# Attention's q and k projected already turned, with the rotary halves moved to 32 partitions and back by DMA

## What is computed

```python
aq = partial_rotary(aq.reshape(B, S, n_heads, ATT_HEAD_DIM), pos)   # n_heads = 24, head 64, S = 512
ak = partial_rotary(ak.reshape(B, S, n_heads, ATT_HEAD_DIM), pos)
...
def partial_rotary(t, pos):
    half = ROT_DIM // 2                                             # ROT_DIM = 16
    ...
    r1 = tf[..., :half]
    r2 = tf[..., half:ROT_DIM]
    out = jnp.concatenate([r1 * cos - r2 * sin, r2 * cos + r1 * sin, tf[..., ROT_DIM:]], axis=-1)
```

## Time and profile before

| | |
|---|---|
| median of 3 runs | 1821.55 us (1821.44 to 1821.83) |
| the profiled execution | 1821.84 us |
| span of its instructions | 1820.0 us, so 1.84 us lie around it |
| TensorE busy in the span | 1790.7 us, 98% |
| VectorE, ScalarE | 1381.0 us (76%), 1100.2 us (60%) |
| `attention_stage`, to the last matmul of v0 | 213.5 to some 356 us from the start |

### The profile page before, as it was taken

How to read it: one execution, slowest core, us unless ns; L and a number is a source line. 1 busy time by engine, 2 the same in 40 slices (tenths; PEclk the granted TensorE clock), 3 DMA queues, 4 the chain that set the end, 5 groups by cost and what they waited for, 6 DMA issues and landing times.

```text
span 1820.0 us, 25032 instructions
## 1 busy us (share of the span) xinstructions
PE 1790.7 (98%) x9119; PEld 1472.9 (81%) x9120; DVE 1381.0 (76%) x1265; ACT 1100.2 (60%) x994; POOL 141.1 (8%) x120
## 2 busy tenths in 40 slices
PE   9999999999999999999999999999999999999996
PEld 7877788898888877788888888888888888888885
DVE  4256344337323568999999999999999999999997
ACT  4253222238331346777777777777777777777774
POOL 1000000000000017110000000000000000000001
PEclk9999999999999999999999999999999999999998
DMA  5321322211323558999999999999999999999993
GB/s 187 124 92 47 127 94 92 84 56 56 120 93 139 180 229 305 378 389 379 383 372 368 387 376 373 381 386 368 380 380 375 373 387 376 373 389 375 375 382 124
DMA packets 100601, 493.95 MB, mean 271 GB/s; under 512 B 15562, under 2 KB 17610, under 8 KB 51008
## 3 DMA queue, kind: packets, MB, share of 16 engines
q1 hardware_dynamic: 90640, 475.97, 68.3%
q0 software_dynamic: 9616, 16.62, 3.6%
q10 hardware_dynamic: 288, 0.59, 0.1%
HBM read 484.40 MB, written 25.21 MB: 280 GB/s over the span
## 4 chain that ended last, share of the span: by engine, by line
PE 58%; POOL 1%; DMA 1%; issue 1%; DVE 1%; ACT 0%; DVEq 0%; POOLq 0%
PE psum L1881 24%; PE psum L1894 12%; PE psum L1884 12%; PE psum L1899 6%; POOL slots_of_experts L1759 1%; PE psum L1853 1%; PE psum L1845 1%; PE psum L1874 1%; DMA h_sb<-normed_rows,row_index 1%; DMA slots_of_experts<-choice_token_and_weight,choice_row_of_table 0%; DMA lists_of_experts<-slots_of_experts 0%; DVE expert_chunk L2032 0%; DVE h_sb L2200 0%; DVE expert_lo L1729 0%; ACT expert_hi L1724 0%
## 5 line engine op out<-in xcount | busy, mean ns | idle before, releaser
L1729 DVE TENSOR_TENSOR expert_lo<-expert_chunk,expert_hi 128x2048 fp32r<-128x2048 f32 x384 | 865.7, 2284 | 45.2 <-ACT expert_hi L1724 42.6
L1724 ACT CAST expert_hi<-expert_chunk 128x2048 fp32r<-128x2048 f32 x384 | 734.9, 1916 | 225.8 <-PE psum L1884 187.6
L275 DVE TENSOR_TENSOR chunk_lo<-chunk,chunk_hi 128x2048 fp32r<-128x2048 f32 x48 | 109.9, 2290 | 252.9 <-ACT chunk_hi L271 252.7
L1881 PE MATMUL psum<-expert_hi,rowsT_hi 128*128 128x512 f32 x992 | 272.0, 396 | 0.0
L1884 PE MATMUL psum<-expert_lo,rowsT_hi 128*128 128x512 f32 x992 | 265.5, 389 | 0.5 <-DVE expert_lo L1729 0.5
L1881 PE MATMUL psum<-expert_hi,rowsT_lo 128*128 128x512 f32 x992 | 265.6, 389 | 0.0
L1884 PEld LDWEIGHTS psum<-expert_lo,rowsT_hi 128*128 128x128 f32 x992 | 186.1, 188 | 40.0 <-DVE expert_lo L1729 1.4
L1881 PEld LDWEIGHTS psum<-expert_hi,rowsT_lo 128*128 128x128 f32 x992 | 186.2, 188 | 39.6
L1881 PEld LDWEIGHTS psum<-expert_hi,rowsT_hi 128*128 128x128 f32 x992 | 181.5, 188 | 41.9 <-issue 7.6
L271 ACT CAST chunk_hi<-chunk 128x2048 fp32r<-128x2048 f32 x48 | 91.8, 1912 | 185.5 <-PE psum L306 158.1
L306 PE MATMUL psum<-chunk_hi,xT_hi 128*128 128x512 f32 x480 | 189.2, 394 | 4.3 <-ACT qk_rows_then_probsT L1070 1.7
(11 more groups left out here) (299 smaller groups left out, 1888.2 us busy)
## 6 DMA issues: line engine op xcount, KB each, us to landing
expert_chunk<-in_expert_w_gate_up SPq DMA_DIRECT2D x256, 1024.0 KB, 7.8
expert_chunk<-in_expert_w_down SPq DMA_DIRECT2D x128, 1024.0 KB, 6.9
chunk<-in_w_in SPq DMA_DIRECT2D x38, 1024.0 KB, 5.0
chunk<-in_w_branch_gla SPq DMA_DIRECT2D x4, 1024.0 KB, 5.0
chunk<-in_w_mix_out SPq DMA_DIRECT2D x4, 1024.0 KB, 5.1
gla_v<-in_x SPq DMA_DIRECT2D x4, 512.0 KB
y_glaT_away<-h_sb SPq DMA_DIRECT2D x1, 2048.0 KB, 7.7
att_qT_then_y_glaT<-y_glaT_away SPq DMA_DIRECT2D x1, 2048.0 KB, 7.6
```

The costliest lines, as they stand in the source:

```text
L275: dve.tensor_tensor(self.wlo[c][:], self.raw[c][:], self.whi[c][:].bitcast(F32), ALU.subtract).then_inc(self.lo_done[c], 1)
L1724: act.copy(self.expert_hi[c % self.SLOTS][:], self.expert_ring[c % self.RING][:]).then_inc(self.moe["hi"], 1)
L1729: dve.tensor_tensor(self.expert_lo[s][:], self.expert_ring[c % self.RING][:], self.expert_hi[s][:].bitcast(F32), ALU.subtract).then_inc(se ...
L1881: pe.matmul(bank, x[:, k, :], whi[s][:, m // 2, m % 2 * COLS:(m % 2 + 1) * COLS], start=False, stop=False)
```

## The change

The six q/k groups are multiplied with the weights stationary (`weights_stay`), as other groups of this kernel are, so a bank holds 128 columns on partitions and the 512 tokens along it. ScalarE copies the bank straight to `q`, `k` or `near`, sorted by residue where wanted (`out`). TensorE's transposes, VectorE's small rotations and its copies from banks 4 to 7 are gone.

The rotary halves now lie on four runs of 8 partitions (0, 8, 64, 72), where partners are on different partitions. So for each group, when its four banks are copied out, ScalarE's queue issues 8 DMAs of 8 partitions by 1024 numbers (`take_halves`, 32 KB each) that lay them out on 32 partitions in `halves`; VectorE multiplies with cosine and sine and adds, in four operations on 32 partitions (`rotate`); and SP issues 8 DMAs that put the result back (`put_halves_back`). The buffer `halves` is one, so the DMAs of group i wait until those that put group i - 1 back have landed (`put_back`). The cosine and sine and both products lie in `att_v`, which is not yet in use; ScalarE's first copy of v0 therefore waits for the sixth rotation (`rotated`).

```diff
@@ gla_stage, tensor engine
-                self.multiply_group(pe, base_att, self.block_of, between=last_turns)
+                self.multiply_group(pe, base_att, None, weights_stay=True, between=last_turns)
@@ attention_stage
+        halves = halves_and_pT[0:turning, :].rearrange("p (m n) -> p m n", n=SEQ)
+        rope, by_cos, by_sin = v[0:turning, 1], v[0:turning, 2], v[0:turning, 0]
+        places = ((q_near, 0), (q, 0), (q, HALF_KT), (k_near, 0), (k, 0), (k, HALF_KT))
...
+        def halves_of(i):
+            qk, at = places[i]
+            for h in range(2):
+                for tile in (0, 2):
+                    part = (h * 2 + tile // 2) * HALF
+                    for s in range(2):
+                        row = h * HEAD_DIM + s * HALF
+                        yield (qk[row:row + HALF, at + tile:at + tile + 2, :],
+                               halves[part:part + HALF, 2 * s:2 * s + 2, :])
@@ SP
-                sp.dma_start(rope[:], t["rope"].rearrange("(b p) n -> p b n", p=P)).then_inc(rope_in, 16)
+                sp.dma_start(rope, t["rope_T"]).then_inc(rope_in, 16)
...
-                with sp.Fori(2, 3 * G + 1) as i:
-                    self.load_group(sp, base + i, lambda c: self.w_in_chunk(COL_AQ + COLS * i)(c))
+                def load(i, c):
+                    sp.wait_ge(self.lo_done[c], base + i)
+                    sp.dma_start(self.raw[c][:], self.w_in_chunk(COL_AQ + COLS * i)(c)).then_inc(self.loaded[c], 16)
+
+                def put_halves_back(i):
+                    sp.wait_ge(rotated, i + 1)
+                    for rows, half_rows in halves_of(i):
+                        sp.dma_start(rows, half_rows).then_inc(put_back, 16)
+
+                load(2, 0)
+                load(2, 1)
+                load(3, 0)
+                for i in range(2 * G):
+                    put_halves_back(i)
+                    load(i + 3, 1)
+                    load(i + 4, 0)
+                load(3 * G, 1)
@@ tensor engine
-                with pe.Fori(1, 2 * G) as i:
-                    qk_group(i, lambda: turn_rows(i - 1))
-
-                self.multiply_group(pe, base_v, self.block_of, between=lambda: turn_rows(2 * G - 1))
+                self.run_groups("multiply", pe, base, (1, 2 * G), weights_stay=True)
+                self.multiply_group(pe, base_v, self.block_of)
@@ scalar engine
+                def out(i):
+                    qk, at = places[i]
+                    for b in range(NB):
+                        act.wait_ge(self.bank_full[b], base + i + 1)
+                        place, tile = qk[:, at + b, :], self.bank[b]
+                        if i % G:
+                            place, tile = place.rearrange("p (r n) -> p r n", r=RES), tile.rearrange("p (n r) -> p r n", r=RES)
+                        act.copy(place, tile).then_inc(self.bank_free[b], 1)
+
+                def take_halves(i):
+                    for b in range(NB):
+                        act.wait_ge(self.bank_free[b], base + i + 1)
+                    if i:
+                        act.wait_ge(put_back, 16 * MOVES * i)
+                    for rows, half_rows in halves_of(i):
+                        act.dma_start(half_rows, rows).then_inc(taken, 16)
+
+                out(0)
                 self.split_hi(act, base + 1, 1)
...
+                take_halves(0)
+                for i in range(1, 2 * G):
+                    self.split_hi(act, base + i + 1, 0)
+                    out(i)
+                    self.split_hi(act, base + i + 1, 1)
+                    take_halves(i)
...
+                    if i == 0:
+                        act.wait_ge(rotated, 2 * G)
@@ vector engine
+                def rotate(i):
+                    order = 2 if i % G else 0
+                    cos, sin = rope[:, order, :], rope[:, order + 1, :]
+                    dve.wait_ge(taken, 16 * MOVES * (i + 1))
+                    dve.wait_ge(rotated, i)
+                    dve.tensor_tensor(by_cos, halves, cos.unsqueeze(1).to_broadcast([turning, 4, SEQ]), ALU.mult).then_inc(products, 1)
+                    sines = sin.unsqueeze(1).to_broadcast([turning, 2, SEQ])
+                    dve.scalar_tensor_tensor(out=by_sin[:, 0:2, :], in0=halves[:, 2:4, :], scalar=-1.0, in1=sines,
+                                             op0=ALU.mult, op1=ALU.mult).then_inc(products, 1)
+                    dve.tensor_tensor(by_sin[:, 2:4, :], halves[:, 0:2, :], sines, ALU.mult).then_inc(products, 1)
+                    dve.wait_ge(products, 3 * (i + 1))
+                    dve.tensor_tensor(halves, by_cos, by_sin, ALU.add).then_inc(rotated, 1)
 
                 self.split_lo(dve, base + 1, 1)
...
+                for i in range(2 * G):
+                    self.split_lo(dve, base + i + 2, 0)
+                    rotate(i)
+                    self.split_lo(dve, base + i + 2, 1)
```

More of the change, by code:

```diff
@@ L61, in shape_constants @@
     cos, sin = np.cos(ang).astype(np.float32), np.sin(ang).astype(np.float32)
-    c["rope"] = np.concatenate([cos, cos, -sin, sin], axis=1).astype(np.float32)
+    by_residue = np.arange(SEQ).reshape(SEQ // RES, RES).T.reshape(-1)
+    c["rope_T"] = np.stack([np.tile(a[order].T, (ATT_HEADS // 2, 1)) for order in (np.arange(SEQ), by_residue) for a in (cos, sin)],
+                           axis=1).astype(np.float32)
     t, r = np.arange(P), np.arange(RES)
@@ L919, in attention_stage @@
         self.groups = base_gate = base_v + G
[L920 to L923, removed]
+        rope_in, taken, products, rotated, put_back, masks_in = (self.sem("att_" + n) for n in (
+            "rope_in", "halves_taken", "rope_products", "rotated", "halves_put_back", "masks_in"))
         q_near, k_near = near
@@ L969, in _ @@
             def _(pe):
[L970 to L978, removed]
                 def score(j):
@@ L1029, in values @@
                     last.then_inc(S["pv_done"], 1)
-                def qk_group(i, before=None):
-                    self.multiply_group(pe, base + i, self.block_of, between=before)
                 def gate_blocks(c, blocks):
@@ L1064, in _ @@
             def _(act):
[L1065 to L1070, removed]
-                self.split_hi(act, base + 1, 1)
[L1072 to L1083, removed]
+                def out(i):
[14 more added lines that the diff above has]
+                out(0)
+                self.split_hi(act, base + 1, 1)
+                take_halves(0)
[4 more added lines that the diff above has]
+                    take_halves(i)
                 def exps(m):
@@ L1129, in _ @@
                 dve.wait_ge(rope_in, 16)
[L1131 to L1156, removed]
@@ L1158, in _ @@
-                self.split_lo(dve, base + 1, 1)
-                rotate(0, q_near)
-                for first, qk in ((0, q), (G, k)):
-                    if first:
-                        for c in range(2):
-                            self.split_lo(dve, base + first + 1, c)
-                        rotate(first, k_near)
-                    with dve.Fori(1, G) as i:
-                        for c in range(2):
-                            self.split_lo(dve, base + first + i + 1, c)
-                        rotate(first + i, qk, i - 1)
+                def rotate(i):
[10 more added lines that the diff above has]
+                    dve.tensor_tensor(halves, by_cos, by_sin, ALU.add).then_inc(rotated, 1)
@@ L1188, in probs @@
                     dve.tensor_scalar(neg[u], neg[u], inv[:, u:u + 1], None, ALU.mult).then_inc(S["probs_done"], 1)
-                with dve.Fori(2 * G + 1, 3 * G) as i:
-                    for c in range(2):
-                        self.split_lo(dve, base + i, c)
+                for c in range(2):
+                    self.split_lo(dve, base_gate - 1, c)
                 self.split_lo(dve, base_gate, 0)
```

10 lines of the change are left out of this document (5 added, 5 removed).

## The result

The changed kernel takes 1829.5 us (median of 6 runs, 1828.2 to 1831.4) against 1821.5: a ratio of 1.0043, with a 95% interval of 1.0032 to 1.0053. It is slower by some 8 us, where 8 us less was forecast, and just above the range. The profiled execution took 1828.66 us with a span of 1826.9, so its own difference from before is 6.9 us of span; the medians lie 8.0 apart.

A forecast was written before the change was run, and what follows sets the result against it. TensorE, busy 98% of the span, was taken as the bound. From 1821.84 us, -10.6 for transposes and +2.5 for a new wait at v0 gave 1813.7, less 0.3: 1813.4 us; range 1811.3 to 1829.

The forecast's parts named there:

- What went: TensorE's 16 transposes in each of six q/k groups disappear, 1.77 us a group: -10.6 us.
- The rotation: VectorE's four rotation operations per group take 7.1 us; fewer partitions save nothing.
- The landing: The last of eight DMAs put back lands 2.1 us after its issue has passed; 3.5 instead would be worth +7.
- The issue price: Each small DMA issue on SP or ScalarE costs 0.50 us, so eight take 4.0 us; sixteen a lap.
- the text's own steepness: One more hundredth of a us per issue adds 0.16 us a lap and 0.64 + 0.16 at v0.
- The ring's form: Loop of rounding, rest, rotation, DMAs back, landing and DMAs out: 21.6 us a lap against TensorE's 21.76, just closing.
- its two outlets: TensorE waits at v0, +2.5 us; for chunk_lo in groups q1 to k2 only if the loop is over 6.5 late.
- rival 1: Issues into the ring cost 0.77 us each, lap 26.1 us, like loads into busy queues: 1835 us; chance 0.20.
- signs of being wrong: Eights of 5 us or more, take_halves waiting longer each group, or TensorE waiting for chunk_lo inside q/k groups.
- The start: First lap hangs on q2's chunk 0 load: rounding from 227.5, lateness 2.0 us at first, 1.3 at v0.
- The chances: Whole change: faster 0.68, slower 0.20, the same 0.12; the forecast's 1812 to 1816 had 0.56.
- The rule beside it: Skill page calls issue time usually small beside the DMA; that would give 8 us of room and 1812.1 us.

The follow-up runs named there:

- the run without any new wait: Changed kernel with halves-out DMAs on SP's queue, sine products in the attention-output tile and q2's first load ahead of the store: 1812.01 us, ratio 0.9943.
- run 8: Changed kernel with sine products in their own place and ScalarE's eight DMAs moved behind the next group's chunk 0 rounding: 1821.23 us, ratio 0.9993.
- run 1: Changed kernel with the sine products in the attention-output tile, so v0's first copy no longer waits for the sixth rotation: 1819.95 us, ratio 0.9987.
- run 2: Changed kernel with the eight DMAs out of q and k issued by SP instead of ScalarE: 1814.33 us, ratio 0.9951.
- run 5: Changed kernel with only the first head of each pair moved and rotated, four DMAs each way, timing only: 1812.64 us, ratio 0.9949.
- run 9: Changed kernel with sine products apart, ScalarE's DMAs behind the next rounding, and SP's loads held until the halves out landed: 1813.01 us, ratio 0.9948.
- run 4: Kernel before plus five sets of four 32 KB DMAs on SP: issues about 0.6 us SBUF to SBUF, 0.3 to 0.4 from HBM; no kernel time given.
- Run 3: Changed kernel with q2's chunk 0 load issued ahead of the tables, the 2 MB store and the masks: 1826.67 us, ratio 1.0023.
- run 7: Changed kernel with halves-out DMAs split four each on ScalarE and SP, sine products apart and q2's first load early: 1811.92 us, ratio 0.9945.

## Why the prediction was wrong

**What went: right.** 10.6 us were forecast for the transposes; the run without any new wait gained 10.8 in the stage.

**The rotation: right.** 7.1 us forecast; 234.65 to 241.5 is 6.9, on 32 partitions and on 16 alike.

**The landing: right, where nothing else is in flight.** 2.1 was taken; 1.8 is measured. That it may meet a load and land late was in the text as harmless, and in this kernel it was; in run 8, where the halves stand last in the ring, it cost 8 us.

**The issue price: the step that failed.** "I take 0.50: 4.0 us" came from rows that all had HBM at one end; the DMAs here, with SBUF at both ends, cost 0.66, and eight of them 5.3 us. By the text's own steepness, 0.8 us for each hundredth, 0.16 more is 12.8 us: 1826.2 for 1813.4. The ring's form and its two outlets (waits for `chunk_lo`, and the wait at v0) are what runs 1, 2, 5 and 9 confirm. It was rival 1 in effect, at a price between the forecast's and its own 0.77, but not for its reason. Full queues are not what made the issues dear: behind the first group all sixteen from `att_kT` took 0.631 or 0.632 us on ScalarE's queue, and SP's, with no load just ahead, a median of 0.625. The rival's remark that no row was a DMA from SBUF to SBUF was the right one; the 8 partitions in it were not what counted (run 4). Two of the signs of being wrong came, the eights of over 5 us and the waits for `chunk_lo`.

**The start: mis-sized.** q2's load was taken to land at 227.5; ScalarE got it at 230.5. Run 8, in which the first eight DMAs are issued only at 227.22, has it when the forecast said:

```profile
227.08 1.91 ACT L273 CAST chunk_hi<-chunk 128x2048 fp32r<-128x2048 f32 x1 [9.73 <-DMA chunk<-in_w_in]
```

So the eight DMAs in flight beside the load cost it 3.4 us, where 0.7 was allowed for them and the larger tables together; they were slow to issue there too (8.0 us from 215.73, for 5.3). Run 3 shows that a start is handed through one for one as far as v1's first matmul, so 3 us more: 1829.2.

**The clock: not in the sum.** After the 9.0 us idle TensorE ran at half its clock for some 3.5 us, 1.8 us lost. Price, start and clock together would give about 1831; the landing was 0.3 and the rotation 0.2 us quicker than forecast in each of five passes, which makes 1828.5, and the restarts, some 1 us, were not in the sum either. That is near the measured 1829.5; closer than 1 us this account does not go.

**The chances.** Twenty in a hundred for slower, at a point where one price unknown in the trace moved the time by 0.8 us per hundredth, was too little. The nearest rows were all of another kind (HBM at one end), and their spread of 0.43 to 0.52 was taken for the spread of the unknown. The bound on the other side, 0.77, was in the text, but with the argument against it that the transfers are small. In run 4 transfers of one size, 32 KB, cost 0.6 or 0.3 to 0.4 by where their ends lie.

**The rule beside it.** The page of the Trainium skill, "DMA: Bandwidth & Descriptors", section Issuing engines are not separate DMA queues, calls the sequencer's time for an issue usually small relative to the DMA. Here eight issues take 5.3 us and the last lands 1.8 later; the measurement decides. Its other half, that issuing from several engines saves only that time, agrees with run 7: the issues took 3.0 us in place of 5.3, and the time stayed.

## What to carry to other kernels

When work leaves the bounding engine, draw the ring that the new buffer makes (who waits to write it, who waits to read it) and add up every queue's time in it, issues too; when the slack is less than a tenth of the lap, one price read off the wrong kind of row decides the sign. If the ring is too long, first look what stands in it without need: here a rounding behind a wait on ScalarE's queue (run 2), loads sent ahead of the halves (run 9), and a scratch place that ties the last lap to a bank (run 1). The first of these alone turned a loss of 8 us into a gain of nearly 9.

## What the runs showed that I had not expected

- Issuing a DMA of 32 KB with SBUF at both ends holds SP for a median of 0.59 to 0.64 us, whether 8, 16 or 128 partitions, and one from HBM for 0.29 to 0.43 (run 4). Only loads were tried on the HBM side; the stage's own store of 2 MB held SP for 0.42. Why is open.
- A few DMAs of 32 KB and a load of 1 MB in flight together delay each other: the first eight cost the load 3.4 us (run 8 against the changed kernel), and behind loads the small ones land 3.5 to 4.1 us after the last issue and not 1.8 (runs 4 and 8, against 9).
- Two queues that issue such DMAs at once hardly slow each other: 0.62 on SP, a median of 0.71 on ScalarE (run 7).
- TensorE came back from a wait of 9.0 us at the lower of its clocks, and from one of 1.7 us (run 2) at the higher. The length of the wait alone does not settle it: in run 1 a wait of 1.88 us ended at 306.51, and from 307.1 to 310.1 matmuls started 0.43 us apart in place of 0.23; the changed kernel had 1.97 us at the same place and kept its clock. Why is open. In the changed kernel behind the 9.0 us (windows, PEclk third from the end of a row):

```profile
360.00:362.00 2.00, 1.05 (x3) 0.91 (x4) 0.19 (x1) 1.78 (x4) 0.00 (x0) 0.50 0.13 16
362.00:364.00 2.00, 2.00 (x6) 1.61 (x5) 0.00 (x0) 2.00 (x2) 0.00 (x0) 0.50 0.35 49
364.00:366.00 2.00, 2.00 (x9) 1.88 (x8) 1.90 (x1) 0.07 (x1) 0.00 (x0) 0.92 0.33 49
366.00:368.00 2.00, 2.00 (x11) 2.00 (x10) 0.39 (x1) 0.00 (x0) 0.00 (x0) 1.00 0.36 58
```

0.50 is 1.2 GHz of 2.4: three and six matmuls in 2 us, then eleven.
